# The first FFN gets seven block products per pair, and the state-space tables move beside its down projections

## The chip, the cores and the metric

One Trainium2 chip, one core. The metric is the device time of one execution in microseconds (us). The engines are PE (matrix products), DVE, ACT and Pool (elementwise work), and SP, which issues DMAs.

## The reference

A decoder trunk of two layers over 1024 tokens of width 1024, fp32, all in one launch. Each layer is a mixer and a feed-forward network:

```
x = x + mixer(rms_norm(x))        # layer 0: RWKV-7 || RG-LRU, layer 1: S5 with a GLU behind it
x = x + conv_ffn(rms_norm(x))

def conv_ffn(xn, w_up, conv_w, conv_b, w_down):
    h = causal_dwconv(xn @ w_up, conv_w, conv_b)     # D_FF = 2816, 3 taps
    gate, val = jnp.split(h, 2, axis=-1)
    return (jax.nn.silu(gate) * val) @ w_down
```

The S5 mixer needs tables that depend only on its parameters: powers of the complex decay of each state, their products with B and C, filters of the first taps, and turns (rotations). They can be computed at any time before it.

## The kernel before

**Products.** Activations lie with channels on partitions and tokens on the free axis: a tile is 128 channels x 1024 tokens. An fp32 product is three products in a rounded format, hi x hi, hi x lo and lo x hi, each in two halves of 512 columns: 6 matmuls for a tile of weights (128 x 128) against a tile of activations. Weights come from DRAM as chunks of up to four tiles (`Dense.load`, L175, on SP), ACT casts the high part (`take_hi`, L190), Pool subtracts for the low part (`take_lo`, L197), PE multiplies (`unit_products`, L1715). There is one slot for each chunk; `w_loaded`, `w_hi_done`, `w_lo_done`, `w_used` and `unit_free` are the counters. A unit is one output tile: 8 input tiles for an up or out projection, n hidden tiles for a down projection over a group of n. DVE adds each finished down unit to the residual stream (`residual_add_dve`, L2950). Every engine runs its own queue in the order written out by hand.

**The first FFN** (`Ffn`, L1903). 22 hidden tiles in groups of 6, 5, 5 and 6. For each tile of a group PE computes the gate's and the value's up unit (48 matmuls each), ACT and DVE scale, convolve and gate (L2194), then 8 down units run over the group and add to the residual.

**The second FFN** (`Fast`, L2274) has two phases. In the first, each of 22 pairs (a gate and a value tile) takes seven block products of 12 matmuls (L2516) in place of 96 matmuls, after sums of blocks of the activations (`sum_blocks`) and of the weights (Pool), with snapshots of partial results on ACT (`snap_act`) and additions on DVE (`evac_dve`). Each hidden tile goes to DRAM (`hidden_sp`). In the second phase the down projections (L2592) run in groups of 8, 6 and 8 tiles; SP fetches the tiles (`fetch_sp`), ACT makes their high part (`h_hi_act`, L2703), DVE the low part (`h_lo_dve`, L2708), and DVE adds to the residual (L2938). Units 0 and 1 of a group run interleaved by chunks, cast in `chunk_hi` (L2719) and `chunk_lo` (L2661). The fetches of the next group's tiles stand one behind each load of down weights.

**The tables** (`Tables`, L3022). `angles_dve` and `angles_act` stand beside the tiles of group 0 of the first FFN, `setup_dve(0..7)` (L3160 on) beside its down units, with `keep_c` (L3096) and transposes of C. Setup 7 ends with memsets (L3217, L3218), which count up `s5_clear`; the first half waits for it. Then come 16 halves, in the down units 2 to 7 of groups 1 and 2 and in the first two up units behind each. A half is:

- `half_pool`: t_mg (L3232), then t_gx (L3239), which waits until PE is done with the half before
- `half_dve`: `states_dve` (L3295), then `powers_dve` for the next (L3285)
- `half_pe`: transposes of t_gx, products k0 and k1; waits for t_gx, the states and `t_kept` of the half before
- `first_act`: `keep_states` (a DMA, L3358), t_first (L3334), d_diag (L3337)
- `half_act`: t_in (L3345), t_fir (L3349, L3352), `keep_filters` (two DMAs, L3364, L3365)

`turns_pool(n)` (L3251, operations L3263 to L3266), 16 of them, stand beside up products of groups 1 and 2; `keep_turns_sp` stores them.

## Time and profile before

| what | value |
|---|---|
| time, median of 3 runs | 2602.37 us (2601.37 to 2604.17) |
| time of the profiled execution | 2604.17 us |
| its span | 2602.4 us |
| mean granted clock of PE | 0.988 |
| PE busy | 2513.5 us, 97% |
| DVE, ACT, POOL busy | 1382.2, 1017.1, 1098.8 us |

The span goes from the first to the last instruction of the core. Shares are of the span. A wait of an engine is shown as idle time before an instruction, with the instruction that released it. Engines other than PE are busy for about half of the time, and where they stand before PE in a chain their order matters.

### The profile page before, as it was taken

The page shows a single profiled execution, that of the slowest core. Times are in us where ns is not written, and L with a number is a line of the kernel's source. Part 1 is how long each engine was busy: PE and PEld are TensorE (multiplying, and loading weights), DVE is VectorE, ACT ScalarE, POOL GpSimd, SP SyncE. Part 2 cuts the span into 40 slices and gives each one's busy share as a digit, 9 for nine tenths or more (in the row PEclk, how much of TensorE's full clock was granted, in tenths as well). Part 3 has the DMA queues.
Part 4 walks back from the last instruction along what each step waited for, and adds up shares of the span by engine and source line. Part 5 has one row for each costly group of instructions (what it writes and reads, how often), then busy time and mean ns, then how long its engine had stood idle before and what let it go on. Part 6 is the DMA issues. An engine that isn't in the chain of part 4 may idle for free.

```text
span 2602.4 us, 34139 instructions
## 1 busy us (share of the span) xinstructions
PE 2513.5 (97%) x13125; PEld 2098.4 (81%) x13125; DVE 1382.2 (53%) x1792; ACT 1017.1 (39%) x1607; POOL 1098.8 (42%) x966
## 2 busy tenths in 40 slices
PE   8999899999999999999999999989999999999997
PEld 6788788888788887788788888978878888878786
DVE  6442478777535564564654436644375565672223
ACT  5443344544333313343343334422264454551222
POOL 5323445453222225566662221112367777752221
PEclk8999999999999999999999999999999999999998
DMA  3111000000113111242241134531212222243222
GB/s 105 45 43 58 18 1 1 1 1 1 50 44 69 47 51 61 83 169 72 91 160 49 45 104 163 197 111 49 64 49 89 73 89 82 81 137 103 79 75 85
DMA packets 246611, 188.59 MB, mean 72 GB/s; under 512 B 24742, under 2 KB 228040, under 8 KB 244424
## 3 DMA queue, kind: packets, MB, share of 16 engines
q1 hardware_dynamic: 232263, 164.95, 20.5%
q10 hardware_dynamic: 14208, 21.76, 2.3%
q8 instruction: 90, 1.47, 0.2%
q14 instruction: 50, 0.40, 0.0%
HBM read 141.58 MB, written 40.89 MB: 70 GB/s over the span
## 4 chain that ended last, share of the span: by engine, by line
PE 62%; issue 5%; DVE 3%; POOL 3%; DMA 1%; ACT 1%; SPq 0%; POOLq 0%; DVEq 0%; ACTq 0%
PE acc_o L1715 30%; PE acc_o L2516 8%; PE bank_a L2516 4%; PE bank_b L2592 4%; PE bank_a L2592 3%; PE bank_b L2516 3%; PE acc_o L1972 2%; POOL dense_lo L197 2%; PE acc_o L2960 1%; PE bank_a L3684 1%; PE bank_b L3707 1%; DMA h_f<-hidden 1%; PE bank_b L3316 1%; PE bank_b L3321 1%; PE bank_a L3307 1%
## 5 line engine op out<-in xcount | busy, mean ns | idle before, releaser
L197 POOL TENSOR_TENSOR dense_lo<-dense_raw,dense_hi 128x512 fp32r<-128x512 f32 x230 | 297.0, 1292 | 812.7 <-ACT dense_hi L190 811.3
L190 ACT CAST dense_hi<-dense_raw 128x512 fp32r<-128x512 f32 x230 | 134.2, 585 | 524.5 <-PE acc_o L1715 384.0
L1715 PE MATMUL acc_o<-a_hi,dense_hi 128*128 128x512 f32 x1008 | 314.2, 393 | 6.0 <-POOL dense_lo L197 3.7
L1715 PE MATMUL acc_o<-a_lo,dense_hi 128*128 128x512 f32 x1008 | 311.8, 391 | 0.0
L1715 PE MATMUL acc_o<-a_hi,dense_lo 128*128 128x512 f32 x1008 | 311.4, 390 | 0.0
L1715 PEld LDWEIGHTS acc_o<-a_hi,dense_hi 128*128 128x128 f32 x1008 | 187.5, 189 | 47.2 <-issue 3.6
L1715 PEld LDWEIGHTS acc_o<-a_hi,dense_lo 128*128 128x128 f32 x1008 | 189.9, 188 | 40.0
L1715 PEld LDWEIGHTS acc_o<-a_lo,dense_hi 128*128 128x128 f32 x1008 | 189.9, 188 | 39.9
L403 PE MATMUL main_ps<-rounded 128*128 128x256 f32 x896 | 128.1, 294 | 8.9 <-DVE rounded L298 8.9
L2194 DVE TENSOR_TENSOR acc_o<-acc_o,spread 128x1024 f32<-128x1024 f32 x44 | 54.2, 1232 | 155.0 <-PE acc_o L1715 149.0
L403 PEld LDWEIGHTS main_ps<-rounded 128*128 128x128 f32 x896 | 113.6, 190 | 27.4 <-DVE rounded L298 23.3
L197 POOL TENSOR_TENSOR w_lo_e<-w_raw_e,w_hi_e 128x512 fp32r<-128x512 f32 x42 | 56.4, 1344 | 158.1 <-ACT w_hi_e L190 158.1
L1715 PE MATMUL acc_o<-c_hi,dense_hi 128*128 128x512 f32 x360 | 112.4, 393 | 4.8 <-POOL dense_lo L197 4.8
L1715 PE MATMUL acc_o<-c_lo,dense_hi 128*128 128x512 f32 x360 | 111.1, 390 | 0.0
L1715 PE MATMUL acc_o<-c_hi,dense_lo 128*128 128x512 f32 x360 | 110.9, 389 | 0.0
L2950 DVE TENSOR_TENSOR x_res<-x_res,acc_o 128x1024 f32<-128x1024 f32 x40 | 48.8, 1221 | 112.6 <-PE acc_o L1715 88.9
L219 PE MATMUL acc_e<-xn_hi_e,w_hi_e 128*128 128x512 f32 x320 | 100.9, 397 | 0.7 <-POOL w_lo_e L197 0.6
L219 PE MATMUL acc_e<-xn_lo_e,w_hi_e 128*128 128x512 f32 x320 | 98.6, 389 | 0.0
L219 PE MATMUL acc_e<-xn_hi_e,w_lo_e 128*128 128x512 f32 x320 | 98.5, 389 | 0.0
L1468 DVE SCALAR_TENSOR_TENSOR p_even<-acc_e,prm,p_even 128x1023 f32<-128x1023 f32 (+2 forms) x25 | 32.1, 1282 | 121.4 <-ACT p_even L1254 121.1
L1715 PEld LDWEIGHTS acc_o<-c_hi,dense_hi 128*128 128x128 f32 x360 | 66.5, 188 | 19.6 <-POOL dense_lo L197 4.2
L1715 PEld LDWEIGHTS acc_o<-c_hi,dense_lo 128*128 128x128 f32 x360 | 67.6, 188 | 14.3
(563 smaller groups left out, 5864.9 us busy)
## 6 DMA issues: line engine op xcount, KB each, us to landing
dense_raw<-in_f_w_up SPq DMA_DIRECT2D x88, 256.0 KB, 3.0
w_raw<-in_f_w_up SPq DMA_DIRECT2D x88, 256.0 KB, 2.9
dense_raw<-in_f_w_down SPq DMA_DIRECT2D x72, 256.0 KB, 2.8
hidden<-val SPq DMA_DIRECT2D x22, 512.0 KB, 2.6
h_f<-hidden SPq DMA_DIRECT2D x22, 512.0 KB, 4.4
w_raw_e<-in_e_w_in SPq DMA_DIRECT2D x42, 256.0 KB, 2.9
s_states<-t_hx ACTq DMA_DIRECT2D x16, 512.0 KB, 2.9
g_in<-s_inputs SPq DMA_DIRECT2D x8, 1024.0 KB, 5.1
```

The costliest lines, as they stand in the source:

```text
L190: nc.scalar.copy(self.hi[:, par, 0:n, :], self.raw[:, par, 0:n, :]).then_inc(w_hi_done, 1)
L197: pool.tensor_tensor(self.lo[:, par, 0:n, :], self.raw[:, par, 0:n, :], self.hi[:, par, 0:n, :].bitcast(F32), op=ALU.subtract).then_inc(w_ ...
L219: last = nc.tensor.matmul(acc[:, h * HALF:(h + 1) * HALF], w[:, par, j, :], x[:, k + j, h * HALF:(h + 1) * HALF], start=first, stop=final)
L403: return nc.tensor.matmul(bank[:, at:at + 2 * CH], lhs, rhs, skip_group_check=True, **flags)
L1468: return nc.vector.scalar_tensor_tensor(out=here, in0=dn.acc[slot][:, 0:SEQ - back], scalar=scale, in1=here, op0=ALU.mult, op1=ALU.add)
L1715: last = nc.tensor.matmul(acc[:, h * HALF:(h + 1) * HALF], w[:, chunk, j, :], x[:, k + j, h * HALF:(h + 1) * HALF], start=first, stop=final)
L1972: last = nc.tensor.matmul(dn.acc[s][:, h * HALF:(h + 1) * HALF], w[:, s, t, :], x[:, k + t, h * HALF:(h + 1) * HALF], start=begin, stop=final)
L2194: nc.vector.tensor_tensor(acc[:, :], acc[:, :], spread[:, :], ALU.mult).then_inc(f_scaled, 1)
L2516: last = nc.tensor.matmul(bank, w[n % 4][:, j, :], x(j, BLOCK[k]), start=begins and j == 0 and w is self.ring_hi and x == self.x_hi, stop= ...
L2592: last = nc.tensor.matmul(self.down_acc[s][:, h * HALF:(h + 1) * HALF], place[w][:, t, :], x[here][:, h * HALF:(h + 1) * HALF], start=begi ...
L2950: nc.vector.tensor_tensor(here, here, dn.acc[slot][:, :], ALU.add).then_inc(unit_free, 1)
L2960: last = nc.tensor.matmul(acc[:, h * HALF:(h + 1) * HALF], w[:, place, j, :], x[:, k, h * HALF:(h + 1) * HALF], start=first, stop=final)
```

## The change

The class `Ffn` of before is deleted, and `Fast` takes its name and does both layers, with offsets for the counters of the second. The first FFN's groups are now 7, 5, 5 and 5 tiles, its down units accumulate in bank_a and bank_b, and the tables use the other accumulator's places. The activations' block sums for the first FFN are made beside the units of the out projection, whose last two units run interleaved by halves (`halves_products`), as those of the GLU did before.

The tables' places are new:

- `angles_dve` and `angles_act` in pair 0 and beside pairs 2 to 7, `setup_dve(0..2)` beside pairs 8 to 10
- group 0's down units: the clearing of t_gx behind unit 1, `setup_dve(3..7)` behind units 2 to 6, keep_c behind 3 and 5, `powers_dve(0)` behind 7; the transposes of C behind units 2 and 4 on PE
- one half beside each of the eight down units of groups 1 and 2
- turn 0 in unit 7 of group 0, turns 1 to 6 in units 1, 4 and 7 of groups 1 and 2, turns 7 to 15 in group 3; on Pool each stands between the two chunks' low parts (behind the half, if there is one)

In both layers: the snapshot u2 comes before p5, the snapshot p5 of pair 0 waits for the norm's sums, the cast of chunk 1 of group 0 stands earlier on ACT, and SP fetches the tiles of the next group earlier (four at once in group 0; in the other groups three between the loads of chunk 0 and chunk 1, then up to two behind each load). In a group of fewer than eight next tiles, tile number c-2 is converted beside unit c.

```
             self.load_chunk(sp, 0, 0)
-            for m in range(8):
+            for m in range(self.groups[0][1]):
                 self.fetch_sp(sp, m)
             self.hidden_sp(sp, NP - 2)
             self.load_chunk(sp, 0, 1)
+            if self.tables:
+                self.tables.load_first_sp(sp, self.q_used0 + SEVEN * NP)
             for g in range(len(self.groups)):
-                if g:
+                fetched = list(self.next_tiles(g))
+                if g == 0:
+                    for m in fetched[:4]:
+                        self.fetch_sp(sp, m)
+                    self.hidden_sp(sp, NP - 1)
+                    fetched = fetched[4:]
+                else:
                     self.load_chunk(sp, g, 0)
+                    if self.tables:
+                        self.tables.beside_sp(sp, g, 1)
+                    for m in fetched[:3]:
+                        self.fetch_sp(sp, m)
                     self.load_chunk(sp, g, 1)
+                    fetched = fetched[3:]
                 for c in range(2, DT):
                     self.load_down(sp, g, c)
...
+                    for m in fetched[:2]:
+                        self.fetch_sp(sp, m)
+                    fetched = fetched[2:]
+                    if self.tables:
+                        self.tables.beside_sp(sp, g, c)
...
             for g, (first, n) in enumerate(self.groups):
-                self.chunk_lo(pool, g, 0)
-                self.chunk_lo(pool, g, 1)
-                for c in range(2, DT):
-                    self.dn.take_lo(pool, n, self.down_unit(g) + c, 0)
+                for c in range(DT):
+                    if c < 2:
+                        self.chunk_lo(pool, g, c)
+                    else:
+                        self.dn.take_lo(pool, n, self.down_unit(g) + c, 0, 0, 1)
+                    if self.tables:
+                        self.tables.beside_pool(pool, g, c)
+                    if c > 1:
+                        self.dn.take_lo(pool, n, self.down_unit(g) + c, 0, 1, 2)
...
                 for c in range(DT):
+                    if self.tables:
+                        self.tables.beside_first_act(act, g, c)
                     if c == 0:
-                        self.chunk_hi(act, g, 1)
+                        if g:
+                            self.chunk_hi(act, g, 1)
                         self.dn.take_hi(act, n, down + 2, 0, 0, 1)
...
+                    if self.tables:
+                        self.tables.beside_act(act, g, c)
+                    for m in self.made_beside(g, c):
+                        self.h_hi_act(act, m)
...
             for g in range(len(self.groups)):
                 for c in range(DT):
+                    if self.tables:
+                        self.tables.beside_first_dve(dve, g, c)
                     unit, par = (self.down_unit(g) + c, 1) if c else (self.down_unit(g) + 1, 0)
                     self.dn.wait_unit(dve, unit, par)
                     here = x_res[:, c, :]
                     nc.vector.tensor_tensor(here, here, self.down_acc[c % 2][:, :], ALU.add).then_inc(unit_free, 1)
...
+                    for m in self.made_beside(g, c):
+                        self.h_lo_dve(dve, m)
+                    if self.tables:
+                        self.tables.beside_dve(dve, g, c)
...
+        HALF_GROUPS = (1, 2)
+        TURNS = {(0, 7): (0,), (1, 1): (1,), (1, 4): (2,), (1, 7): (3,), (2, 1): (4,), (2, 4): (5,), (2, 7): (6,),
+                 (3, 0): (7,), (3, 1): (8,), (3, 2): (9,), (3, 3): (10,), (3, 4): (11,), (3, 5): (12,), (3, 6): (13,),
+                 (3, 7): (14, 15)}
...
+        def beside_pool(self, pool, g, c):
+            if self.half_of(g, c) is not None:
+                self.half_pool(pool, self.half_of(g, c))
+            for n in self.TURNS.get((g, c), ()):
+                self.turns_pool(pool, n)
+
+        def beside_pe(self, pe, g, c):
+            if (g, c) in ((0, 2), (0, 4)):
+                self.turn_c_pe(pe, c // 2 - 1)
+            if self.half_of(g, c) is not None:
+                self.half_pe(pe, self.half_of(g, c))
...
+        def beside_dve(self, dve, g, c):
+            if g == 0 and c == 1:
+                nc.vector.memset(t_gx[:, :, :, :, :], 0.0).then_inc(s5_clear, 1)
+            elif g == 0 and c == 7:
+                self.powers_dve(dve, 0)
+            elif g == 0 and c > 1:
+                if c in (3, 5):
+                    self.keep_c(dve, c // 2 - 1)
+                self.setup_dve(dve, c + 1)
```

## Rows read from the trace of the kernel before

**Rows 1.** The page: busy us (share of the span) xinstructions.

```profile
PE 2513.5 (97%) x13125; PEld 2098.4 (81%) x13125; DVE 1382.2 (53%) x1792; ACT 1017.1 (39%) x1607; POOL 1098.8 (42%) x966
```

**Rows 2.** The chain that ended last: start us, us, engine and line, instructions.

```profile
1116.57 6.86 PE acc_o L1715 x30
...
1488.85 54.40 PE acc_o L1715 x240
...
1927.37 19.04 PE acc_o L2516 x84
```

**Rows 3.** Timeline of DVE: start us, us, line, operation, [idle before <-releaser].

```profile
754.15 1.22 DVE L2950 TENSOR_TENSOR x_res<-x_res,acc_o 128x1024 f32<-128x1024 f32 x1 [6.02 <-PE acc_o L1715]
...
942.50 1.40 DVE L3096 COPY c_s<-bank_b 64x512 f32<-64x512 f32 x2
...
950.73 0.09 DVE L3207 MEMSET fine<- 128x32 f32 x1
...
973.34 0.48 DVE L3218 MEMSET t_fir<- 128x512 f32 x1
...
1097.13 3.21 DVE L3295 TENSOR_TENSOR t_hx<-t_mh 64x288 f32<-64x288 f32 x4 [1.66 <-PE bank_b L3321]
...
1101.82 0.45 DVE L3285 TENSOR_TENSOR t_mh<-c_neg,power 128x288 f32<-128x288 f32 x1
```

**Rows 4.** Timeline of PE: same columns.

```profile
982.02 1.22 PE L1715 MATMUL acc_o<-a_hi,dense_hi 128*128 128x512 f32 x2 [2.68 <-POOL dense_lo L197]
...
2341.43 0.72 PE L2592 MATMUL bank_a<-h_hi,dense_hi 128*128 128x512 f32 x2 [3.34 <-POOL dense_lo L2661]
...
2445.08 0.70 PE L2592 MATMUL bank_b<-h_hi,dense_hi 128*128 128x512 f32 x2 [2.69 <-DVE x_res L2938]
```

**Rows 5.** Busy us (xinstructions) of each engine by window, granted clock, DMA.

```profile
754.00:1537.80 783.80, 775.29 (x3625) 643.77 (x3624) 424.25 (x554) 265.25 (x444) 342.29 (x376) 1.00 0.26 78
1899.80:1927.30 27.50, 23.87 (x106) 17.64 (x105) 23.29 (x18) 14.87 (x24) 19.48 (x12) 1.00 0.10 29
1927.00:2322.00 395.00, 395.00 (x1744) 327.10 (x1743) 236.00 (x232) 202.01 (x295) 308.59 (x228) 1.00 0.28 91
2430.00:2513.00 83.00, 77.61 (x332) 62.91 (x331) 20.87 (x17) 18.95 (x27) 21.34 (x18) 0.98 0.32 99
2445.00:2450.00 5.00, 4.92 (x15) 3.94 (x16) 0.00 (x0) 0.00 (x0) 0.62 (x1) 0.66 0.63 184
```

**Rows 6.** Timeline of ACT beside one down unit with a half.

```profile
1104.48 1.07 ACT L3345 COPY t_in<-bank_a 128x512 f32<-128x512 f32 x2
1105.98 1.21 ACT L3349 COPY t_fir<-bank_b 32x64 f32<-32x64 f32 x4 [0.42 <-PE bank_b L3316]
...
1107.97 0.45 ACTq L3365 DMA_DIRECT2D s_filters<-t_fir  x1
...
1110.73 0.71 ACT L3334 COPY t_first<-t_gx 128x256 f32<-128x256 f32 x2 [3.14 <-POOL t_gx L3239]
1111.34 0.53 ACT L3337 ACTIVATE d_diag<-eye,d_rows 128x32 f32<-128x32 f32 x2
```

**Rows 7.** Timeline of POOL, a turn and a half.

```profile
1062.00 0.62 POOL L3263 TENSOR_TENSOR t_rot<-fine,coarse 128x256 f32<-128x256 f32 x1
...
1065.13 0.75 POOL L3266 TENSOR_TENSOR t_rot<-t_rot,t_tmp 128x256 f32<-128x256 f32 x1
...
1103.38 1.29 POOL L197 TENSOR_TENSOR dense_lo<-dense_raw,dense_hi 128x512 fp32r<-128x512 f32 x1 [1.80 <-ACT dense_hi L190]
...
1107.10 3.59 POOL L3239 TENSOR_TENSOR t_gx<-t_mg 64x256 f32<-64x256 f32 x4
1110.77 0.56 POOL L197 TENSOR_TENSOR dense_lo<-dense_raw,dense_hi 128x128 fp32r<-128x128 f32 x1
```

**Rows 8.** Groups of instructions by line: busy, mean ns of one, idle before.

```profile
L2708 DVE TENSOR_TENSOR h_lo<-h_f,h_hi 128x1024 fp32r<-128x1024 f32 x22 | 31.5, 1438 | 36.8 <-ACT h_hi L2703 36.8
...
L2703 ACT CAST h_hi<-h_f 128x1024 fp32r<-128x1024 f32 x22 | 22.7, 1046 | 32.4 <-DMA h_f<-hidden 32.4
```

More of the change, by code:

```diff
@@ L2258, in trunk @@
+    f_start, f_tap, f_silu, f_h, f_hi, f_lo = (
+        sem("f_" + n) for n in ("start", "tap", "silu", "h", "hi", "lo"))
     NP = FT
@@ L2327, in down_unit, with param, pair_chunks @@
+            self.c_hi = [here(f"h_hi{k}", [P, SEQ], hi, F32R) for k, (hi, lo) in enumerate(places)]
+            self.c_f32 = [here(f"h_f32_{k}", [P, SEQ], lo) for k, (hi, lo) in enumerate(places)]
+            self.c_lo = [here(f"h_lo{k}", [P, SEQ], lo, F32R) for k, (hi, lo) in enumerate(places)]
         def down_unit(self, g):
             return self.u0 + DT * g
+        def param(self, at_, tile):
+            return prm[:, tile + at_:tile + at_ + 1]
+        def pair_chunks(self, g):
+            return [(self.down_unit(g) + j, k, n) for j, (k, n) in enumerate(self.dn.chunks(self.groups[g][1]))]
@@ L2572, in products_pe @@
                         last.then_inc(w_used, 1)
-                    if g == len(self.groups) - 1:
+                    if self.tables:
+                        self.tables.beside_pe(pe, g, c)
+                    if g == len(self.groups) - 1 and self.turns:
                         if c == 2:
@@ L2628, in begin_sp, with next_tiles @@
                 self.load_raw(sp, 0, n)
+        def next_tiles(self, g):
+            first, n = self.groups[g + 1] if g < len(self.groups) - 1 else (FT, 0)
+            return range(first, first + n)
         def load_sp(self, sp):
@@ L3416, in trunk @@
         nm_out = OutNorm(dn.acc)
-        pair_banks = ((bank_a, bank_b), (dn.acc[0], dn.acc[1]))
-        ffn1 = Fast(1, dn, (bank_a, bank_b), nm2, nm_out, ((0, 8), (8, 6), (14, 8)), pair_banks, Dense.u + 2)
+        h_places1 = ([place for n in range(SEVEN) for place in (tiles(C_AT, 2 * n, 2 * n + 1), tiles(A_AT, third[n], fourth[n]))],
+                     [*range(14), *range(8)], [("product", k // 2) for k in range(14)] + [("group", 0)] * 8)
+        ffn1 = Ffn(1, dn, (bank_a, bank_b), nm2, nm_out, ((0, 8), (8, 6), (14, 8)), pair_banks, C_AT, A_AT, E_AT, h_places1, turns=True)
         sig = (gate, val)
```

726 lines of the change are left out of this document (256 added, 470 removed).

## The prediction

> **What bounds the kernel now.** I read the busy table first: PE is busy for 97% of the span [rows 1], so a matmul less is time less wherever PE has no wait of its own. Then the chain that ended last: it runs through PE both in the stretches of the first FFN and in the pair loop of the second, and gives the pitch of a 512-column matmul: 240 of them in 54.40 us and 84 in 19.04 us, both 0.2267 us [rows 2]. A down unit with a half of the tables behind it takes 9.74 us: 6.86 of it are the 30 matmuls of five tiles, 2.88 the half on PE [rows 2].
>
> The first FFN's stretch on PE runs from the last product of the out projection (the residual addition of its last tile starts at 754.15 [rows 3]) to the 216th matmul of the chain's group that starts at 1488.85 [rows 2], 1537.8: 783.8 us. Its content is 3168 matmuls (44 up units of 48, 176 tile products of 6 for the down projections) x 0.2267 = 718.1, sixteen halves x 2.88 = 46.1, the sums of the norm 3.7 and the transposes of C and of the s rows 2.4: 770.3. So 13.5 us are waits and the clock's reaction to them. The window over it agrees roughly: PE busy 775.3 of 783.8 [rows 5].
>
> The second FFN already has the form that the first is to get. In its pair loop PE is busy in 395.00 of 395.00 us, with DVE at 236.00, ACT at 202.01 and POOL at 308.59 [rows 5]: pairs of seven block products are bound by PE alone. Its waits sit elsewhere: at the entry (PE busy 23.87 of 27.5 [rows 5]), at the boundary between the phases (3.34 on the first lo part [rows 4]), and in the second down group, where the fetched hidden tiles come late (2.69 before one unit [rows 4]; such waits sum to 5.4 there: 83.0 us of which PE is busy 77.61 [rows 5]).
>
> **The change, part by part.**
>
> *Products.* Seven blocks of 12 matmuls replace 96 matmuls per pair: 22 x 12 = 264 fewer. 264 x 0.2267 = **-59.8**. The waits that the old first FFN had go with its order: **-13.5**. What follows is what comes in their place.
>
> *Entry and pair loop.* The entry of the second FFN leaves PE idle 3.6 us [rows 5]; the first gets the same entry, with its last out unit cut into halves. I take **+3.2** for it, and +0.5 for the halved products of the out projection. Beside the pairs stand the angles (20 small copies, 6.0 us on DVE) and setups 0 to 2 (3 to 4.3 us). DVE has (395.0 - 236.0) / 20.7 pairs = 7.7 us free per pair, so these cost nearly nothing: **+0.5**. Without that cover they would cost their length, some 25 us.
>
> *Group 0 (seven tiles, units of 42 matmuls = 9.52 us, setups 3 to 7 on DVE).* A boundary wait of **+1.2**, below the second FFN's because the cast of chunk 1 is earlier. Then one chain, counted from the end of unit 4. Setup 5 can start at 2.8, after a residual addition of 1.22 [rows 3] and an h_lo of some 1.4 [rows 8]. From its start at 950.73 to the last memset of setup 7, which starts at 973.34 and takes 0.48, the trace of before shows 23.1 us with one residual in it [rows 3]. The new order puts two h_lo (2 x 1.23), a keep_c (1.40 [rows 3]) and one residual more (1.22) between: 2.8 + 23.1 + 5.1 = 31 us. Only then are the tables clear, and turns_pool(0) waits for that on Pool. It takes 3.9 us (from 1062.00 to 1065.88 [rows 7]), and chunk 1 of unit 7 (three tiles, 1.0 us) is queued behind it: 35.8. PE asks for that chunk after units 5 and 6 and four tiles, 9.52 x 2 + 5.44 + 1.0 of slack = 25.5. **+10.3**. The same instruction had no product queued near it before. Behind it wait PE and, through the slots, ACT's casts and SP's loads of group 1.
>
> *Groups 1 and 2 (five tiles, a half beside each unit).* PE's content is 8 x 9.74 per group. What may be longer is a loop that ACT and DVE close. In the new order the next group's hidden tile is cast on ACT behind half_act(c), its lo part stands on DVE between residual(c) and states(c+1), and first_act(c+1) waits for states(c+1) before half_pe(c+1) can finish. Link by link: casts of the next weights 0.85 (my estimate for a four-tile and a one-tile one), t_in 1.07, t_fir 1.21 [rows 6], bank_b's copy and two DMA issues to 1108.42, 1.2 after t_fir [rows 6], h_hi 1.05 [rows 8], h_lo 1.3 (mean 1.44 [rows 8], least 1.2), states, then the issue of the states' DMA 0.4, t_first 0.71 and d_diag 0.53 [rows 6]. The states took 3.21 us for four operations while gx ran on Pool, against 0.45 for one operation of the same 288 elements on DVE by itself [rows 3]. In the new order gx (3.59 [rows 7]) starts at the end of half_pe and is over before h_lo is, so the states should meet less of it: I take 4 x 0.45 = 1.8, and 3.2 for the range. The sum is 10.1, with 0.5 for the crossings between engines 10.6, against 9.74: +0.9 for a unit with a hidden tile (five per group, one of which carries a turn: 4 x 0.9 = 3.6).
> Turns stand on Pool behind half_pool and ahead of lo chunk 1. Gx can start only when half_pe(c-1) has ended; 3.6 + 3.9 + 0.6 for the last lo [rows 7] is 8.1 after it, PE then has 1.4 of its unit and 2.9 of its half left: 12.3 instead of 9.74, +2.5 for units 4 and 7 of each group: 5.0.
> At a group's start PE alone would run chunk 0 of units 0 and 1 (10.9), half 0 (to 13.8), chunk 1 of both (16.5) and half 1 (19.4). But ACT's cast for unit 2 stands ahead of half_act(0) and waits for unit 0's chunk 1, at 15.1; with the cast half_act(0) ends at 19.3, first_act(1) at 20.9, and half_pe(1), which waits for both, some 2.0 later: +3.5. Unit 2 comes in 2.0 longer than 9.74 behind it, because its half_act starts late too: +5.5 in all. Together 14.1 per group, **+28.2**. With the states at 3.2 it is 1.4 x 10 = 14 more; if the loop stays under 9.74 it is 7 less, and if the start is hidden as well, 18 less.
>
> *Group 3 (five tiles, turns 7 to 15).* Content 54.4. turns(8) stands before the lo part of unit 2: 3.9 us late, 3.4 of it seen. With one slot per chunk, cast 0.62 and lo 1.29 [rows 7] stand against 1.36 us of the one-tile chunk: a gap of 0.8 in five units, 4.0 in all. Turns 14 and 15 in the last unit, before its last lo part: +3.0 and a rest of 0.2. **+10.6**. The loads of the next weights stand on SP behind the keeping of turns 14 and 15: **+3.5** at the S5 mixer's projection.
>
> *The clock.* After an idle of 2.68 us PE's next two matmuls took 1.22 us [rows 4] where two pitches are 0.45, and it lost 1.4 in all, by my count of the stretch; the windows behind the idle of 2.69 show a granted clock of 0.66, which is half speed for most of 5 us [rows 5]. Five of the new waits are that long (two group starts, the tables' wait, two in group 3): 5 x 1.4 = **+7.0**. If every turn and every hidden tile did this it would be up to 14 more; if none did, 7 less.
>
> *The second FFN.* Fetching three tiles between the first two chunk loads takes the late tiles away: **-5.4**. The cast of chunk 1 moved up takes 2.0 of the 3.34 at the boundary: **-2.0**; the rest is the lo part itself. The order of the snapshots costs nothing: no product that follows directly reads p5's copy. Both could be 0 if the queue of DMAs, not their place, makes the tiles late.
>
> Sum: -59.8 - 13.5 + 3.7 + 0.5 + 1.2 + 10.3 + 28.2 + 14.1 + 7.0 - 7.4 = **-15.7**. The profiled execution took 2604.17 us (span 2602.4), the median is 2602.37; off the median this gives 2586.7, rounded **2587**.
>
> The Trainium skill, "SBUF — State Buffer", section "Who interferes with whom", says that a DVE instruction with two inputs in SBUF contends with a GpSimd instruction that reads SBUF. The states beside gx (3.21 against 4 x 0.45) agree. By that rule alone any DVE addition of the tables or of h_lo that still meets gx or mg would be stretched, and the sum would go to the third rival's.
>
> **The rivals.**
> (1) *As summed*: most of the gain is given back in the down groups, 2575 to 2598.
> (2) *The beside-work is hidden*: DVE, ACT and Pool are each under 60% busy, and the groups' waits come out at a third: -28 for the loops, the starts and group 3, -5 of the clock: about 2555. Against it: the order in each queue is fixed, and turns and hidden tiles are in front of what PE needs.
> (3) *Slower: DVE and Pool hold each other up in groups 1 and 2.* h_lo meets gx (up to 2.30 for one instead of 1.3: +1.0), the states still do (+1.4), and PE's clock falls in each of the ten units (+1.4): 3.8 x 10 = +38, 2625. The point from which the change is slower by more than 5.2 us is a loop of 10.6 + 2.1 = 12.7 us. For it: the lo parts' mean of 1.44 with least 1.2 shows that such meetings happen. Against it: mg and gx themselves were hardly stretched [rows 7].
> (4) *The pair loop of the first FFN isn't PE's*: tables beside seven of the pairs each hold back a snapshot by 3 us: +21, 2608. The second FFN's loop with 7.7 us free on DVE speaks against it.
>
> **Numbers.** What a measurement here tells from no change is about 0.2%, 5.2 us: 2597.2 to 2607.6. Chances: (1) 0.50, nearly all faster; (2) 0.15, faster; (3) 0.23, of which 0.05 ends within 0.2%; (4) 0.12, most within 0.2%. With 0.05 of (1) within it: faster 0.60, same 0.19, slower 0.21. Range 2562 to 2617; the likeliest case alone 2575 to 2598.
>
> **What would show it.** A pair loop without idle in the first FFN, too, at 19.04 us a pair; PE's idle before unit 7 of group 0, released by the lo part behind turns_pool, of some 10 us; periods of 10.6 and 12.3 us in the chain in groups 1 and 2, with ACT (d_diag, t_first) as releaser; the states' time there; no idle on a residual in the second FFN's second group. Wrong it would be if the periods there are 9.74 (then 2), or 12 and more (then 3), or if DVE's setups stretch when Pool's sums of the pairs run beside them.

## The result: 30 us slower, and where the trace of the changed kernel puts them

The changed kernel takes 2631.82 us (median of 4 runs, 2627.27 to 2632.25) against 2601.87 us of the kernel before on the same chip: ratio 1.0114, 95% interval 1.0100 to 1.0129. The prediction's 2587 and its range up to 2617 are both missed, and the sign with them. The profiled execution has a span of 2630.3 us, 27.9 more than before.

The page first: busy us, share and instructions, then the granted clock in 40 slices.

```profile
PE 2481.5 (94%) x12861; PEld 2064.8 (78%) x12861; DVE 1473.8 (56%) x1902; ACT 1107.8 (42%) x1782; POOL 1320.7 (50%) x1120
...
PEclk9999999999999999999899889999999999999998
```

PE has 264 matmuls less than in [rows 1] and is busy for 32 us less, and its share falls from 97% to 94%. Before, POOL was busy for 1098.8 us; now it is 1320.7. Three of the five slices from 1249 to 1578 us show a clock of 8 tenths.

The chain that ended last gives the borders of the stages: pair loops, and the first rows of each down group.

```profile
783.20 19.05 PE acc_o L2172 x84
...
1197.25 5.44 PE bank_a L2256 x24
...
1288.41 5.44 PE bank_a L2256 x24
...
1392.36 5.47 PE bank_a L2256 x24
...
1496.52 5.46 PE bank_a L2256 x24
...
1964.36 19.04 PE acc_o L2172 x84
```

The first FFN's pair loop ends at 1197.25, its groups begin at 1197.25, 1288.41, 1392.36 and 1496.52, and the last product ends at 1568.93 (the idle of 2.68 before 1571.61, below). Each stage can now be set against its term. "Content" is matmuls at the pitch of [rows 2] with the halves' 2.88 us.

| stage | content | predicted | measured | off |
|---|---|---|---|---|
| entry and 22 pairs (counted from 754.0) | 422.6 | 426.8 | 443.2 | +16.4 |
| group 0 | 78.3 | 91.2 | 91.2 | 0 |
| group 1 | 77.9 | 93.4 | 104.0 | +10.6 |
| group 2 | 77.9 | 93.4 | 104.2 | +10.8 |
| group 3 | 54.4 | 67.8 | 72.4 | +4.6 |
| to the second FFN's first product (before: 362.0) | | 365.5 | 366.3 | +0.8 |
| second FFN (before: 683.9) | | 676.5 | 675.5 | -1.0 |

(The clock's 7.0 us are shared out as the prediction counted them: 1.4 for each long wait.) The off column sums to 42.2, and -15.7 + 42.2 = 26.5 is the difference of the spans, 27.9, but for 1.4. So the gain is lost mainly in two places: before the first down group, and in the units of groups 1 and 2.

The first row is counted from 754.0, where the kernel before ends its out projection. The changed kernel's first pair product starts at 750.71 in this trace; in the traces of the kernels below, whose code is the same up to there, it starts anywhere from 750.7 to 754.3, so these 3.2 us are no gain of the change. From that product on, the entry (the first pair) takes 9.6 us more than its content of 22.7, where 3.7 was expected, and the 21 pairs behind it take 14.2 more than 21 x 19.04 (783.20 to 1197.25), where 0.5 was. No run isolates the entry: the same code takes from 31.5 to 34.8 us for it in the traces below.

Busy us of the engines in windows over these stages, columns as in [rows 5]:

```profile
784.00:1197.00 413.00, 403.43 (x1761) 331.37 (x1760) 267.59 (x325) 207.24 (x305) 304.10 (x227) 0.99 0.28 89
1211.00:1290.00 79.00, 69.44 (x300) 56.82 (x301) 45.83 (x120) 12.82 (x19) 19.86 (x20) 0.94 0.26 76
1290.00:1396.00 106.00, 88.28 (x459) 74.95 (x458) 66.74 (x86) 40.46 (x109) 82.37 (x105) 0.90 0.49 168
1396.00:1501.00 105.00, 87.19 (x454) 73.94 (x453) 55.02 (x69) 40.51 (x109) 76.25 (x99) 0.92 0.42 147
1501.00:1572.00 71.00, 56.45 (x222) 42.58 (x221) 30.93 (x22) 23.10 (x32) 55.48 (x64) 0.92 0.21 69
2364.00:2611.00 247.00, 245.86 (x1110) 203.63 (x1110) 76.13 (x63) 63.39 (x83) 55.79 (x46) 1.00 0.24 75
```

In the first window PE is idle for 10 of 413 us, where [rows 5] had none in 395. In groups 1 and 2 it is idle for 18 of 106 and of 105 us with a clock of 0.90 and 0.92, and POOL is busy for 78% and 73% there. The last window is the second FFN's down phase, whole: 1.1 us idle in 247, where it took 257 before. PE's longest idles:

```profile
975.01 1.22 PE L2172 MATMUL bank_a<-x_early_l,w_l 128*128 128x512 f32 x2 [4.33 <-POOL w_l L2110]
...
1281.45 1.22 PE L2256 MATMUL bank_b<-h_hi_l,dense_hi 128*128 128x512 f32 x2 [8.04 <-POOL dense_lo L197]
...
1345.95 1.22 PE L2256 MATMUL bank_a<-h_hi_l,dense_hi 128*128 128x512 f32 x2 [6.21 <-POOL dense_lo L197]
...
1566.43 0.80 PE L2256 MATMUL bank_b<-h_hi_l,dense_hi 128*128 128x512 f32 x2 [4.30 <-POOL dense_lo L197]
...
1571.61 1.19 PE L1715 MATMUL acc_o<-a_hi,dense_hi 128*128 128x512 f32 x2 [2.68 <-POOL dense_lo L197]
```

The row at 1345.95 is the pattern of groups 1 and 2: four times per kernel PE waits 5.6 to 6.2 us for the one-tile low part of a unit in which a turn stands on Pool, and then two matmuls take 1.22 us, where a row of two at full clock shows 0.62. The granted clock behind this wait is 0.51, the lower of its two levels, 1.2 and 2.4 GHz:

```profile
1346.00:1352.00 6.00, 6.00 (x22) 5.34 (x23) 1.22 (x1) 1.47 (x3) 3.48 (x5) 0.51 0.34 102
```

**Inside the pair loop.** The stretch of pair 9, in which DVE runs setup 1; first DVE, then POOL:

```profile
961.49 4.11 DVE L2896 TENSOR_TENSOR small<-power 128x32 f32<-128x32 f32 x4
...
965.96 0.50 DVE L2896 TENSOR_TENSOR small<-power 128x32 f32<-128x32 f32 x4
```

```profile
961.76 1.29 POOL L2122 TENSOR_TENSOR w_raw_l<-w_raw_l 128x512 f32<-128x512 f32 x1
963.01 1.29 POOL L2110 TENSOR_TENSOR dense_lo<-w_raw_l,dense_hi 128x512 fp32r<-128x512 f32 x1
964.26 1.29 POOL L2126 TENSOR_TENSOR w_sums_l<-w_raw_l,w_sums_l 128x512 f32<-128x512 f32 x1
973.69 1.27 POOL L2110 TENSOR_TENSOR w_l<-w_raw_l,w_l 128x512 fp32r<-128x512 f32 x1 [8.14 <-ACT w_l L2106]
```

The same four independent instructions on 32 columns take 4.11 us as long as POOL works through its sums and low parts, one after the other at 1.29 us, and 0.50 us when POOL has stopped at 965.55. One by one, the first of the four takes 0.36 and the other three 1.33 each. POOL then idles 8.14 us, because the cast that releases it waits on ACT for an activation that waits for DVE's additions, which stand behind the setup. Setup 1 lasts 7.9 us in this place. At the end of that chain is PE's idle of 4.33 at 975.01.

The durations are not all of it. The copies of pair 2 take 6.4 us (821.71 to 828.1), close to the 6.0 that were counted, and the next pair still lasts 21.9 instead of 19.04. DVE's free time in a pair lies almost whole in one place, ahead of the addition of the later snapshot, and the blocks stand behind that addition:

```profile
819.23 1.30 DVE L2635 TENSOR_TENSOR bank_b<-bank_b,p_kept_later_l 128x512 f32<-128x512 f32 x2 [6.88 <-ACT p_kept_later_l L2369]
```

**Inside a turn unit** (unit 4 of group 1), ACT, POOL, DVE:

```profile
1330.75 0.72 ACT L3142 COPY t_first<-t_gx 128x256 f32<-128x256 f32 x2 [4.14 <-DVE t_hx L3107]
...
1331.80 0.80 ACT L190 CAST dense_hi<-dense_raw 128x512 fp32r<-128x512 f32 x2
```

```profile
1332.48 1.27 POOL L197 TENSOR_TENSOR dense_lo<-dense_raw,dense_hi 128x512 fp32r<-128x512 f32 x1 [3.73 <-ACT dense_hi L190]
1333.71 2.39 POOL L3044 TENSOR_TENSOR t_mg<-b_bar,power 128x256 f32<-128x256 f32 x4
1336.18 4.12 POOL L3051 TENSOR_TENSOR t_gx<-t_mg 64x256 f32<-64x256 f32 x4
1340.38 0.71 POOL L3075 TENSOR_TENSOR t_rot<-fine,coarse 128x256 f32<-128x256 f32 x1
...
1344.34 0.93 POOL L3078 TENSOR_TENSOR t_rot<-t_rot,t_tmp 128x256 f32<-128x256 f32 x1
1345.35 1.78 POOL L197 TENSOR_TENSOR dense_lo<-dense_raw,dense_hi 128x128 fp32r<-128x128 f32 x2
```

```profile
1328.36 1.94 DVE L3107 TENSOR_TENSOR t_hx<-t_mh 64x288 f32<-64x288 f32 x4
...
1338.73 3.47 DVE L3107 TENSOR_TENSOR t_hx<-t_mh 64x288 f32<-64x288 f32 x4
```

The ends of the second product of three halves in a row (1334.29, 1353.29, 1363.54) show that the turn unit lasts 19.0 us and the unit behind it, with a hidden tile and no turn, 10.25:

```profile
1333.23 1.06 PE L3133 MATMUL acc_o<-t_hx,t_gx 128*128 128x128 f32 x8
...
1352.23 1.06 PE L3133 MATMUL acc_o<-t_hx,t_gx 128*128 128x128 f32 x8
...
1362.48 1.06 PE L3133 MATMUL acc_o<-t_hx,t_gx 128*128 128x128 f32 x8
```

ACT casts the weights of unit 4 at 1331.80, behind first_act. So their low part ends at 1333.7 and t_mg at 1336.1, 1.8 us after the half before it ended; t_gx meets h_lo and the states and takes 4.1, the turn takes 4.9 (six instructions of 0.8 against 0.62 in [rows 7]), and the low part that PE needs is done at 1345.9, 11.7 us after the half. The prediction had 8.1.

### The profile page after: what moved, and what is told of

Same layout as the page of the kernel before. It is cut to its first block, busy times and chain, and to the rows that moved or that the text cites. A ratio compares the mean times of both kernels' runs of the same rounds, so it can differ in the third digit from the quotient of the medians.

```text
span 2630.3 us, 33735 instructions
## 1 busy us (share of the span) xinstructions
PE 2481.5 (94%) x12861; PEld 2064.8 (78%) x12861; DVE 1473.8 (56%) x1902; ACT 1107.8 (42%) x1782; POOL 1320.7 (50%) x1120
## 4 chain that ended last, share of the span: by engine, by line
PE 59%; DVE 6%; POOL 5%; issue 2%; ACT 2%; DMA 0%; ACTq 0%; SPq 0%; DVEq 0%; POOLq 0%
PE acc_o L2172 14%; PE acc_o L1715 9%; PE bank_a L2172 8%; PE bank_a L2256 7%; PE bank_b L2256 7%; PE bank_b L2172 6%; PE acc_o L2713 2%; PE bank_a L3526 1%; POOL dense_lo L197 1%; PE bank_b L3549 1%; POOL t_gx L3051 1%; DVE x_late_l L2070 1%; POOL t_rot L3075 0%; DVE t_hx L3107 0%; POOL t_tmp L3075 0%
## 5 line engine op out<-in xcount | busy, mean ns | idle before, releaser
L197 POOL TENSOR_TENSOR dense_lo<-dense_raw,dense_hi 128x512 fp32r<-128x512 f32 (+3 forms) x142 | 178.2, 1256 | 494.4 <-ACT dense_hi L190 492.6
L2110 POOL TENSOR_TENSOR dense_lo<-w_raw_l,dense_hi 128x512 fp32r<-128x512 f32 x88 | 118.3, 1344 | 65.2 <-ACT dense_hi L2106 65.1
L2256 PE MATMUL bank_b<-h_hi_l,dense_hi 128*128 128x512 f32 x352 | 112.7, 402 | 26.0 <-POOL dense_lo L197 25.9
L2110 POOL TENSOR_TENSOR w_l<-w_raw_l,w_l 128x512 fp32r<-128x512 f32 x88 | 115.0, 1306 | 40.9 <-ACT w_l L2106 40.9
L2256 PE MATMUL bank_a<-h_hi_l,dense_hi 128*128 128x512 f32 x336 | 108.5, 405 | 23.7 <-POOL dense_lo L197 22.2
L2172 PE MATMUL acc_o<-x_early_l,dense_hi 128*128 128x512 f32 x352 | 108.8, 390 | 3.3 <-POOL dense_lo L2110 3.3
L2256 PE MATMUL bank_b<-h_lo_l,dense_hi 128*128 128x512 f32 x352 | 110.8, 397 | 0.0
L2256 PE MATMUL bank_b<-h_hi_l,dense_lo 128*128 128x512 f32 x352 | 110.7, 396 | 0.0
L2172 PE MATMUL acc_o<-x_late_l,dense_hi 128*128 128x512 f32 x352 | 108.5, 389 | 0.0
L2256 PE MATMUL bank_a<-h_lo_l,dense_hi 128*128 128x512 f32 x336 | 105.5, 396 | 0.0
```

What stands on the lines that cost most here:

```text
L197: pool.tensor_tensor(self.lo[:, par, 0:n, :], self.raw[:, par, 0:n, :], self.hi[:, par, 0:n, :].bitcast(F32), op=ALU.subtract).then_inc(w_ ...
L2110: pool.tensor_tensor(self.ring_lo[n % 4], self.source(ORDER[n % SEVEN]), self.ring_hi[n % 4].bitcast(F32), op=ALU.subtract).then_inc(q_lo, 1)
L2172: last = nc.tensor.matmul(bank, w[n % 4][:, j, :], x(j, BLOCK[k]), start=begins and j == 0 and w is self.ring_hi and x == self.x_hi, stop= ...
L2256: last = nc.tensor.matmul(self.down_acc[s][:, h * HALF:(h + 1) * HALF], place[w][:, t, :], x[here][:, h * HALF:(h + 1) * HALF], start=begi ...
```

## The experiments

All differences here are under 2%; a kernel is called faster or slower where the interval of its ratio excludes 1. Differences between two kernels are rounded: their medians and their ratios to the kernel before give values up to 2 us apart.

### Turns behind the last low part

```
                     if c > 1:
                         self.dn.take_lo(pool, n, self.down_unit(g) + c, 0, 1, 2)
+                    if self.tables and g in (1, 2):
+                        self.tables.late_pool(pool, g, c)      # turns_pool, taken out of beside_pool
```

> The changed kernel, but in groups 1 and 2 each turn stands on Pool behind the low part of chunk 1 instead of ahead of it. Theory T (in the four turn units of units 4 and 7 the chain on Pool, mg, gx and turn, holds the last low part back: PE idles 6.2 us and then runs at half speed): the periods of 17.5 to 19.0 us fall to about 11, PE's idles of 5.6 to 6.2 go, 4 x 7 = 25 to 30 us less than the changed kernel, about 2604. Rival R (DVE and Pool hold each other up in all units, the turn's place hardly matters): the turn's 4 to 5 us on Pool are paid in the next unit instead, at most 10 us less. By the prediction's own sum a turn unit cost 2.5 us: 10 less.

Measured: 2618.34 us, ratio to before 1.0057 (1.0039 to 1.0076); against 1.0114 that is some 14 us less. Groups 1 and 2 fall by 18 us, from 104.0 and 104.2 to 96.2 and 93.9. Counted from half to half, the turn units shrink from between 17.5 and 19.0 us to between 11.8 and 12.5, but the units behind them grow to 13.5 to 15.0, because the next weights' low part now waits for the turn. PE's idles there are short:

```profile
1353.52 0.70 PE L2256 MATMUL bank_b<-h_hi_l,dense_hi 128*128 128x512 f32 x2 [1.38 <-POOL dense_lo L197]
...
1361.04 0.85 PE L2256 MATMUL bank_b<-h_hi_l,dense_hi 128*128 128x512 f32 x2 [1.80 <-POOL dense_lo L197]
```

Theory T named the place rightly and its size too high: 18 us in the two groups, 14 in all, instead of 25 to 30. The turn's place mattered, and a part of its time moved to the next unit, as R has it.

### Turn 0 out of unit 7 of group 0

```
-        TURNS = {(0, 7): (0,), (1, 1): (1,), ...
+        TURNS = {(1, 0): (0,), (1, 1): (1,), ...
```

> The changed kernel, but turn 0 stands behind half 0 in unit 0 of group 1 instead of in unit 7 of group 0. Theory S (in unit 7 the turn waits for the last memset of setup 7, and the low part of chunk 1 waits behind it): the idle of 8.0 us goes, with the clock's part 9 to 11 us less than the changed kernel. Rival (setup 7 is late anyway: half 0 waits for the same memsets, so the wait goes to the start of group 1): less than 4 us less, and half 0's transposes come later by as much.

Measured: 2625.48 us, ratio 1.0087 (1.0072 to 1.0103), some 7 us less than the changed kernel. Group 0 falls from 91.2 to 80.3 us and the idle of 8.0 is gone; group 1 starts with an idle of 3.3 on t_gx and grows by 3. This is the wait that the prediction priced at 10.3, with 1.4 for the clock: it is 10.9 in all. 3 us of it come back one group later, so that the sum lies between the 9 to 11 of theory S and the 4 of its rival. They do not come from the memsets, which are over at 1280.9, before half 0 asks for them: turn 0 now takes Pool from 1289.27 to 1293.9, ahead of half 1's t_mg and t_gx.

### The pair loop's work in small pieces

```
+            elif 8 <= i < 18:
+                self.small_step(dve, i - 8)     # setups 0 to 2 in ten pieces, angles(0) in four
-            elif i in (8, 9, 10):
-                self.setup_dve(dve, i - 8)
```

> The changed kernel, but the work beside the pairs is cut into small pieces: the copies of angles(0) in four pairs of five, setups 0 to 2 in ten pairs in place of three. The same instructions. Theory L (in the pair loop one long block on DVE, stretched by Pool, runs out of the room of a pair, and the snapshot or addition behind it holds PE back): PE's idles of 1.5, 0.7, 0.8, 4.3 and 0.9 us go, and most of the 14.2 us that the 21 pairs take beyond 21 x 19.04: 10 to 14 us less. Rival (every piece costs what it takes, because DVE has no room in a pair when Pool stretches it): no less, or more.

Measured: 2646.99 us, ratio 1.0172 (1.0157 to 1.0188): 15 us more, not less. From the first FFN's first pair product to its first down product it takes 462.4 us against 446.4; the 21 pairs behind the first take 27.9 more than 21 x 19.04, against 14.4. Theory L is refuted in its remedy: a piece of a setup stands where Pool is in the middle of its run, its first four instructions take 4.1 us together, the whole piece about 4.4, and 13 pairs lose some 2 us each. So a pair absorbs about half of such a piece at this place, although DVE's free time per pair adds up to 7.7 us.

### The same work where Pool is idle

The copies and setups 1 and 2 leave pairs 2, 9 and 10; setup 0 stays at pair 8.

```
+            if g == 0 and c == 0:
+                self.angles_dve(dve, 0)
             elif g == 0 and c == 1:
                 nc.vector.memset(t_gx[:, :, :, :, :], 0.0).then_inc(s5_clear, 1)
+                self.setup_dve(dve, 1)
+                self.setup_dve(dve, 2)
```

> The changed kernel with that last edit alone. In the changed kernel turn 0 waits for setup 7 in unit 7 of group 0, so if the edit makes the setups end later, PE waits as much longer there: the pairs gain 10, group 0 loses what its chain on DVE grows by, of 7 us of work with 4 us of idle to take it: 4 to 8 us less than the changed kernel.

Measured: 2619.23 us, ratio 1.0064 (1.0049 to 1.0079), some 13 us less, where 4 to 8 were expected: the pairs gave back more than the 10, and group 0 did not grow. The pairs with their entry take 433.7 instead of 446.4 us, the 21 behind the first 2.6 more than 21 x 19.04 instead of 14.4; group 0 is 91.4 against 91.2. Setup 1 in its new place, DVE:

```profile
1211.76 0.42 DVE L2898 TENSOR_TENSOR small<-power 128x32 f32<-128x32 f32 x4
...
1212.55 0.49 DVE L2898 TENSOR_TENSOR small<-power 128x32 f32<-128x32 f32 x4
...
1214.80 1.42 DVE L2898 TENSOR_TENSOR power<-small 128x32 f32<-128x32 f32 x2
```

Four instructions take 0.42 to 0.49 us; one pair of them takes 1.42, and there POOL has a low part from 1214.78. The whole setup is over in 5.3 us instead of 7.9. With the run before it this settles the place: the same instructions cost 12 us of the pair loop and nothing in group 0, where Pool is nearly idle. It changes two things at once, Pool beside the instructions and the point of DVE's queue at which they stand; the durations show the first, and no run parts the second from it.

### Half turns, and a turn's share in each unit

Turns 0 to 6 are cut in two (the cosine's three instructions, the sine's three) and laid behind the last low part of units 1 to 7 of groups 1 and 2.

```
+        PARTS = {(1 + k // 7, 1 + k % 7): ((k // 2, k % 2),) for k in range(14)}
```

> The changed kernel with turns 0 to 6 cut in two (three operations of a turn each) and laid behind the low part of chunk 1 in units 1 to 7 of groups 1 and 2, one piece per unit; turn 0 leaves group 0 with that. Theory T2 (Pool idles 1.3 to 3.7 us behind that low part, a piece of 2.0 to 2.5 us fits there, a whole turn of 4 to 5 doesn't): periods near 10.4 in all units, groups 1 and 2 at about 84 to 88 us each instead of 104, group 0 at 80 instead of 91: 40 to 45 us less than the changed kernel, about 2588 to 2592. Rival (Pool is full in these groups, so that any place costs the same): not under the 2612 that the two single edits give together.

Measured: 2602.81 us, ratio 1.0002 (0.9990 to 1.0014): as fast as the kernel before, 29 us less than the changed kernel, where 40 to 45 were expected. Group 0 takes 80.7, groups 1 and 2 take 94.1 and 93.2. The periods are not 10.4 but 11.6 nearly throughout: T2 is wrong about the room behind the low part. It is below the 2612 of the rival, too.

### Fewer turns in group 3

```
+        TURNS = {(3, 0): (7,), (3, 2): (8,), (3, 3): (9,), (3, 4): (10,), (3, 5): (11,), (3, 6): (12,), (3, 7): (13,)}
+        LATE = (14, 15)      # behind the low parts of the projection's unit 0
```

> The same, with turn 8 moved out of unit 1 of group 3 and the last two turns laid behind the first low parts of the S5 mixer's projection, so that one turn stands in each of units 0 and 2 to 7. Theory: the idles of 4.5 and 4.3 us in group 3 go and the one of 2.7 to 3.3 at the projection nearly so; group 3 takes 64 instead of 72: 10 to 14 us less than the run before it. Rival (the projection's first units pay for it, the turn's table being awaited by the first loads of the S5 mixer): under 5 us less.

Measured: 2600.35 us, ratio 0.9998 (0.9986 to 1.0009): no gain that can be told. Group 3 falls from 72.4 to 62.9 us as expected, but from its end to the second FFN's first product it takes 375.6 us instead of 366.3. PE waits there for the S5 mixer's norm. Followed back, the wait does not begin on DVE. DVE's reciprocal waits for the root on ACT, the root stands on ACT behind a cast, the cast waits for weights, and their load stands on SP behind the stores of turns 14 and 15, which wait for Pool; PE, DVE, ACT, and SP's queue:

```profile
1550.39 3.78 PE L1788 MATMUL bank_b<-sq,ones_row 8*128 8x512 f32 x4 [4.57 <-DVE sq L1781]
...
1547.45 0.94 DVE L1777 RECIPROCAL rstd_rows<-rstd_rows 8x128 f32<-8x128 f32 x1 [12.82 <-ACT rstd_rows L1772]
...
1545.12 0.62 ACT L190 CAST dense_hi<-dense_raw 128x512 fp32r<-128x512 f32 x1 [12.55 <-DMA dense_raw<-in_o_w_in]
...
1537.79 4.28 SPq L3102 DMA_DIRECT2D s_turns<-t_rot  x2
1542.12 1.05 SPq L180 DMA_DIRECT2D dense_raw<-in_o_w_in  x2
```

The rival is right that the projection pays: the 9 us come back through the loads of its weights, which wait in SP's queue for the turns to be stored. No run has these loads ahead of the stores.

### All of it with the setups in group 0

> The same, with angles(0) and setups 1 and 2 laid behind units 0 and 1 of group 0, where DVE idles 2.9 and 9.1 us and Pool is nearly idle, instead of beside the pairs. Theory C (Pool holds up each small DVE instruction beside the pairs): the same instructions take under 4.5 us for setup 1 instead of 8, the pairs lose 4 instead of 14 us, group 0 gains 2 at most: 8 to 10 us less, about 2568, which is faster than the kernel before by 1.3%. Rival (group 0's chain on DVE has no room): the loss moves to the start of group 1, 0 to 3 us less.

Measured: 2589.34 us, ratio 0.9948 (0.9934 to 0.9961). The pairs take 437.1 instead of 445.6 us and group 0 80.4 as in the run before it: 11 us less than that run, and faster than the kernel before, by 0.5% instead of the 1.3% that was named; that figure had counted on gains of the two runs above that did not come.

### The second FFN's orders alone

The kernel before, with the fetches and the cast of chunk 1 as in the change.

```
             self.h_hi_act(act, 5)
+            self.chunk_hi(act, 0, 1)
             self.h_hi_act(act, 6)
...
                     self.load_chunk(sp, g, 0)
+                    for m in fetched[:3]:
+                        self.fetch_sp(sp, m)
                     self.load_chunk(sp, g, 1)
```

> The kernel before, with nothing changed but the second FFN's order: tiles fetched earlier on SP, the cast of chunk 1 of group 0 earlier on ACT. As predicted: 7.4 us less than the kernel before, about 2595; the idles of 3.3 and of 2.7, 0.9, 1.0 and 0.8 us go. Rival (the gain of 7.5 in the changed kernel comes from the order of snapshots or from the new class): under 2 us.

Measured: 2593.10 us, ratio 0.9959 (0.9945 to 0.9973): 10 us faster than the kernel before. The down phase takes 246.6 instead of 256.6 us (first product to last), and of its idles only two of 0.5 and 0.6 us are left. The prediction had 7.4 for it; the 2.6 more would be what the clock had taken after those waits ([rows 5] has it at 0.66 behind one of them), but no run separates that.

### What the turns cost in all

Turns 2 to 15 compute one column in sixteen; the rest of their tables is left out.

> The changed kernel with turns 2 to 15 computed for one column in sixteen only (the same instructions and places, next to no time on Pool); it leaves out 15 of 16 parts of these turns. It prices the turns' time on Pool as a whole. Theory T: groups 1 and 2 fall from 104 us each to about 86 (the rest is the starts' 5.5 us and the periods of 10.3), group 3 from 72 to about 62 (the single slots remain), 50 us less than the changed kernel, about 2582. Rival R (the halves and the hidden tiles, not the turns, hold these groups up): at most 20 us less. By the prediction's terms the turns of groups 1 to 3 cost 10 + 7 + 3: 20 less.

Measured: 2608.48 us, ratio 1.0028 (1.0018 to 1.0038), 22 us less than the changed kernel. A turn still takes 2.5 us on Pool in a turn unit (six instructions of 0.3 to 0.5), and three of the four units still last 15.5 us, the last 13.1, with idles of 3.1 to 3.9; group 3 falls to 61.6. By its number the run speaks for R, but it isn't the clean removal that was meant: half of the turn's time stayed. What it shows is a slope: 2.4 us less on Pool ahead of the low part took 2.0 to 3.5 us off three of the turn units and 5.4 off the fourth. It leaves open how much of the rest is the turn's.

### The cast ahead of first_act

```
+                    if early:      # groups 1 and 2, units 2 to 6
+                        self.dn.take_hi(act, n, down + c + 1, 0, 0, 1)
                     if self.tables:
                         self.tables.beside_first_act(act, g, c)
```

> The changed kernel, but in units 2 to 6 of groups 1 and 2 ACT casts chunk 0 of the next unit's weights ahead of first_act(c) instead of behind it. Theory M (the cast stands behind the states' wait and d_diag, so that the low part and t_mg begin 2 us too late and t_gx, which the turn and the last low part stand behind, ends late): Pool's t_mg is over before half_pe(c-1) ends, the turn units of unit 4 and 7 shorten by 2 to 4 us each, the other periods of 10.3 fall to 9.8 to 10.3: 8 to 15 us less than the changed kernel, about 2619. Rival (t_gx waits for half_pe anyway and the order of the cast doesn't matter): under 3 us less.

Measured: 2621.69 us, ratio 1.0067 (1.0050 to 1.0084), 10 us less than the changed kernel by the medians, 12 by the ratios. The turn units last 15.9 to 16.7 us instead of 17.5 to 19.0, the others 10.1 to 10.5 behind the starts, and groups 1 and 2 fall by 9.5 us together. PE's wait in unit 4 of group 1:

```profile
1351.47 1.22 PE L2256 MATMUL bank_a<-h_hi_l,dense_hi 128*128 128x512 f32 x2 [4.72 <-POOL dense_lo L197]
```

It is 1.5 us shorter than the 6.21 of the changed kernel. Theory M holds, at the lower end of its size. This is the link that the prediction's chain of a turn unit left out.

### Turns on DVE, and the version to keep

Turns 0 to 4 stay in pieces in units 2 to 6 of groups 1 and 2, 5 to 11 stand on Pool in group 3, and 12 to 15 run on DVE at the start of group 3.

```
+        PARTS = {(1 + k // 5, 2 + k % 5): ((k // 2, k % 2),) for k in range(10)}
+        TURNS = {(3, 0): (5,), (3, 2): (6,), (3, 3): (7,), (3, 4): (8,), (3, 5): (9,), (3, 6): (10,), (3, 7): (11,)}
+            for n in {(3, 0): (12, 13, 14), (3, 4): (15,)}.get((g, c), ()):
+                self.own_turn_dve(dve, n)
```

> The version with the setups in group 0 and half turns, but with only turns 0 to 4 on Pool in groups 1 and 2 (a piece in each of units 2 to 6), turns 5 to 11 on Pool in group 3, and turns 12 to 15 on DVE at the start of group 3, where DVE idles 14 us, stored to DRAM from places that the tables no longer need. Nothing of them stands at the S5 mixer's projection. Theory: against the version before it the projection and the S5 mixer gain 9 us back (362 to 366 us from the end of the first FFN to the second's first product, instead of 375), groups 1 and 2 gain 1.2 us for each of the four pieces fewer; group 3 stays at 63: 12 to 15 us less, about 2575. Rival (on DVE the turns meet Pool's in group 3 and push its units out): group 3 grows by 5 or more and the sum is 2585.

Measured: 2577.66 us, ratio 0.9910 (0.9893 to 0.9927): faster than both kernels, by 23 us than before. Group 3 is 63.6, the way from there to the second FFN is 364.2, and of the 12 us less than the version before it 11 come from there; groups 1 and 2 stay at 93.8 and 93.5, although they carry four pieces less. The reason can be read in the loop of unit 3, DVE and POOL:

```profile
1316.59 3.43 DVE L3166 TENSOR_TENSOR t_hx<-t_mh 64x288 f32<-64x288 f32 x4
```

```profile
1314.68 4.39 POOL L3066 TENSOR_TENSOR t_gx<-t_mg 64x256 f32<-64x256 f32 x4
...
1319.66 0.84 POOL L3095 TENSOR_TENSOR t_rot<-fine,coarse 128x256 f32<-128x256 f32 x1
```

t_gx and h_lo with the states run at the same time, the states take 3.43 us instead of 1.94, and a piece of a turn follows on Pool. The prediction had such a loop, 12.0 us with the states at 3.2 (10.6 and 1.4 more), and put it aside for the one with 1.8; here it is 11.6.

> The version with turns on DVE, with the same edit. There the periods are 11.6, because t_gx runs until h_lo and the states are on DVE: states 3.4 us, t_gx 4.4. Theory M: t_gx ends before the states begin, they take 1.9, the periods of units 3 to 7 fall to 10.4: some 10 periods x 1.2 = 10 to 12 us less, about 2566. Rival (DVE and ACT close the loop whatever Pool does): no less, and the states still take 3.4.

Measured: 2577.54 us, ratio 0.9901 (0.9884 to 0.9917): the same time. The periods are 11.1 to 11.6, the states still take 3.3. Theory M fails here: t_gx starts 0.3 to 0.9 us earlier behind the half, and Pool is still at work, now with the end of t_gx and the piece behind it, when the states run. The rival's signs came; its reason, that DVE and ACT close the loop whatever Pool does, is not shown, since Pool still meets the states.

## Why the prediction was wrong, point by point

- **The matmuls** (-59.8) and the old waits (-13.5) went as counted: PE's 12861 matmuls are 264 fewer.
- **The pair loop** (+0.5, measured 14.2): this step failed. It took the durations of setups 0 to 2 from places of the kernel before where Pool was nearly idle, and compared them with the sum of DVE's free time in a loop where POOL is busy in 308.59 of 395 us [rows 5]. Setup 1 took 7.9 us instead of some 4. The sum of the free time was the wrong measure too: it lies ahead of one addition, and copies that kept their 6 us still cost the next pair 2.9. The fourth rival had the right place and 21 us as its price, against 14. What showed it are the runs with the same work elsewhere: +15 us in small pieces, -13 us in group 0.
- **The entry** (+3.7): 9.6 from its first product. It was taken over from the second FFN. In the sum the miss is half hidden, since the trace happens to start the first pair 3.2 us early; its cause stays open.
- **Group 0** (+1.2, +10.3, and 1.4 of clock): the cause is right, and the removal of turn 0 shows it. That the sum fits to 0.1 us is in part luck: the wait for the tables with its clock was 10.9 instead of 11.7 (8.04 idle and 2.9 of slow matmuls), the boundary 2.4 instead of 1.2.
- **Units with a hidden tile** (10.6): nearly right. Units 2, 3 and 5 of the groups last 10.0 to 10.4 us, with the states at 1.94 in units 3 and 5. Unit 6, without a turn of its own, lasts 11.3: PE waits 1.24 us for its low part, and the states take 2.89. With the cast ahead it is 10.5.
- **Turn units** (12.3, four of them): mis-sized by 5.2 to 6.7 us each, 24 in all, and it is this term that carries groups 1 and 2. The chain was right, its start and its links were not: the low part and t_mg were taken as over when the half before ends, and they end 1.8 us after it, because the cast stands behind first_act (moving it gives back 0.8 to 2.6 us per unit); t_gx takes 4.1 instead of 3.6 and the turn 4.9 instead of 3.9 while DVE works (t_gx takes 3.16 in unit 5, where DVE is idle for most of it); and after an idle of 6 us PE's last six matmuls and the transposes behind them run at the lower clock level (0.51 granted, above), some 3 us, for which no term stood in these units. The prices of the last three were read from the trace and not separated by a run.
- **The starts** (+5.5): group by group the first halves come with idles of 1.9 and 1.5 to 1.8; what is left of groups 1 and 2 beyond the turn units and the 10.3 of the others fits the term, but no run isolates it.
- **Group 3** (+10.6 and 2.8 of clock): 18.0, low by 4.6. Its waits are those named (4.46 behind turn 8, 0.85 in a unit, 4.30 behind turns 14 and 15), only longer: the two last turns hold PE for 4.3 where 3.0 was said, and the plain units last 7.94 us, 1.1 over their content where 0.8 was said.
- **The clock** (+7.0, five waits of 1.4): mis-sized. Behind the idle of 8.04 it cost 2.9, and behind the four waits of the turn units some 3 each. The two matmuls of 1.22 us were set against two pitches of 0.45; a row of two shows 0.62 at full clock.
- **The projection** (+3.5): 4.3.
- **The second FFN** (-7.4): -8.4 in the changed kernel, -10 alone.
- **The rivals.** The third, slower through DVE and Pool holding each other up at 2625, is the nearest to what happened, but for its place: it had ten units lengthened by 3.8 us each, and in the changed kernel it was four units by 6 and the pair loop. The states at 1.8 came in two halves of each group (1.94); in the other six they took 2.9 to 3.6, 3.47 in the turn unit shown above, where PE waited for the low part and not for them.

The error that the parts share: a duration was read in one neighbourhood and used in another. [Rows 3] held the warning, 3.21 us for four instructions where one alone takes 0.45; it was applied to the states and, in a rival, to h_lo, but not to the setups. The Trainium skill, "SBUF — State Buffer", section "Who interferes with whom", says that a DVE instruction with two SBUF inputs contends with a GpSimd instruction that reads SBUF, and calls the contention for the shared ports an exclusive lock. The trace agrees for the pair loop: three of the four small DVE instructions take 1.33 us each, about one Pool instruction of 1.29. By these rows the price of a block on DVE there goes by the number of its instructions until Pool pauses, not by its busy time.

## What to carry to other kernels

When work is moved beside another engine's stream, read its durations from a place where that stream runs, and count the instructions, not only the microseconds: here small ones paid about one Pool instruction each. Look also where in the loop the free time lies, not only how much there is. A low part, a cast or a load of the next weights is better placed ahead of side work in its queue where an engine waits for it (14 us for the low parts, 10 to 12 for the cast in the changed kernel, nothing for the cast in the last version), and side work is to be priced from the moment at which the queue can really begin it. Before a saving in products is spent, look where the side work has an idle engine next to it: the same 264 fewer matmuls came out at +30 us or -23 us by the place of the tables. Both figures hold the second FFN's new orders, which gave -10 us alone; if the two add up, the first FFN's change is worth some -13 us in the best version.

## What was not expected of the hardware

- Four independent DVE instructions of 128x32 took 4.11 us beside Pool instructions of 1.29 us each and 0.50 us after them. Of the sixteen copies of 32x8 beside pair 2, which read one operand, two took 1.2 us instead of 0.17.
- It works both ways, but less on Pool: the turn's instructions took 0.83 instead of 0.62 us, t_gx 4.1 to 4.4 instead of 3.2.
- A 128x16 instruction on Pool took 0.3 to 0.5 us against 0.8 for 128x256 in the same place: cutting the columns to a sixteenth saved half.
- Two turns on Pool at the S5 mixer's projection cost 9 us through a queue in which they do no work: SP stored them ahead of the next weights, and a cast on ACT waited 12.55 us for that load, with the norm's root behind it.
- After PE's idle of 6.21 us the next six matmuls took 2.7 us instead of 1.4, at a granted clock of 0.51; after an idle of 1.38 the first two took 0.70, no more than the 0.71 at the start of a unit without an idle (at 1334.04 in the changed kernel).
